# Dense products beside the delta rule, issued in portions of four chunks of a tile in place of two

## What is computed

```python
CHUNK, A_HEADS, A_DK, A_DV = 64, 8, 128, 128

def _gated_deltanet(q, k, v, alpha, beta, a_log, dt_bias):
...
    kk = jnp.einsum("bhncd,bhnjd->bhncj", k, k)
    L = jnp.where(strict, beta[..., :, None] * kk * decay, 0.0)
    rhs = jnp.concatenate([beta[..., None] * v, (beta * jnp.exp(G))[..., None] * k], axis=-1)
    sol = lax.linalg.triangular_solve(jnp.eye(CHUNK, dtype=f32) + L, rhs, left_side=True,
                                      lower=True, unit_diagonal=True)
    u_t, w = sol[..., :A_DV], sol[..., A_DV:]
...
    def step(S, inp):
        ut, wt, pt, qt, kt, et = inp
        U = ut - jnp.einsum("bhck,bhkv->bhcv", wt, S)
        o = jnp.einsum("bhck,bhkv->bhcv", qt, S) + jnp.einsum("bhcj,bhjv->bhcv", pt, U)
        S = S * et[..., None, None] + jnp.einsum("bhck,bhcv->bhkv", kt, U)
        return S, o
```

## Time and profile before

| | before |
|---|---|
| median of three runs (lowest, highest) | 2479.69 us (2476.96, 2483.39) |
| profiled execution, its own time | 2473.95 us |
| its span | 2472.3 us |
| busy: PE, PEld, DVE, ACT, POOL | 2425.7, 2004.9, 1007.0, 935.4, 1182.7 us |
| dense matmuls L1886, largest group (HH, WH) | 1992, 795.0 us |
| mean granted clock of TensorE | 0.993 of full |

### The profile page before, as it was taken

One profiled execution on the slowest core, in us unless ns is written; L12 is line 12 of the kernel. 1 busy time (PEld: TensorE's weight loads), 2 busy tenths in 40 slices (PEclk: granted clock), 3 DMA queues, 4 the chain that ended last, 5 costly groups with the idle time before them and its releaser, 6 DMA issues.

```text
span 2472.3 us, 35533 instructions
## 1 busy us (share of the span) xinstructions
PE 2425.7 (98%) x14295; PEld 2004.9 (81%) x14295; DVE 1007.0 (41%) x2261; ACT 935.4 (38%) x1435; POOL 1182.7 (48%) x1566
## 2 busy tenths in 40 slices
PE   8999999999999999999999999999999999999998
PEld 6888888888788888888888888877868887888887
DVE  7974211124874211123867774224345333211113
ACT  5553222224563322224544453235553344322221
POOL 5125655654115565655533233443326645655563
PEclk9999999999999999999999999999999999999999
DMA  5532223224632223224211111232213322223222
GB/s 177 139 103 86 102 88 109 99 77 130 164 103 86 103 81 115 85 85 141 94 58 53 53 52 53 81 133 86 69 58 128 116 96 79 96 86 110 103 80 83
DMA packets 42403, 237.17 MB, mean 96 GB/s; under 512 B 4736, under 2 KB 7936, under 8 KB 19712
## 3 DMA queue, kind: packets, MB, share of 16 engines
q1 hardware_dynamic: 39936, 218.13, 25.0%
q0 software_dynamic: 2304, 16.78, 3.3%
HBM read 213.92 MB, written 4.19 MB: 88 GB/s over the span
## 4 chain that ended last, share of the span: by engine, by line
PE 91%; DVE 4%; POOL 2%; issue 1%; ACT 1%; DMA 1%; SPq 0%; DVEq 0%; POOLq 0%; ACTq 0%
PE PB L1886 75%; PE PB L1888 4%; POOL WL L3028 1%; PE PB L1898 1%; PE PB L1923 1%; PE PB L2136 1%; PE PB L2117 1%; DVE cc L2614 1%; PE PB L1970 1%; PE PB L1987 1%; PE PB L2124 1%; DMA WR<-in_w_in 1%; PE PB L2148 1%; PE PB L2164 1%; PE PB L2087 0%
## 5 line engine op out<-in xcount | busy, mean ns | idle before, releaser
L3028 POOL TENSOR_TENSOR WL<-WR,WH 128x256 fp32r<-128x256 f32 (+1 forms) x1444 | 1055.0, 767 | 753.6 <-ACT WH L2183 753.6
L1886 PE MATMUL PB<-HH,WH 128*128 128x512 f32 x1992 | 795.0, 399 | 11.0 <-ACT HH L2198 10.5
L1886 PE MATMUL PB<-HL,WH 128*128 128x512 f32 x1992 | 779.4, 391 | 0.9 <-DVE HL L2506 0.9
L1886 PE MATMUL PB<-HH,WL 128*128 128x512 f32 x1992 | 516.5, 396 | 0.8 <-DMA WL<-WR 0.8
L2183 ACT ACTIVATE WH<-WR 128x2048 fp32r<-128x2048 f32 (+1 forms) x209 | 371.9, 1779 | 245.9 <-PE PB L1886 238.2
L1886 PEld LDWEIGHTS PB<-HH,WH 128*128 128x128 f32 x1992 | 375.8, 189 | 101.2 <-issue 13.7
L1886 PEld LDWEIGHTS PB<-HL,WH 128*128 128x128 f32 x1992 | 375.8, 189 | 76.9 <-issue 1.7
L1886 PEld LDWEIGHTS PB<-HH,WL 128*128 128x128 f32 x1992 | 366.4, 188 | 75.3 <-issue 2.0
L1886 PE MATMUL PB<-BL,WH 128*128 128x512 f32 (+1 forms) x859 | 331.6, 387 | 0.6 <-DVE BL L2515 0.6
L1886 PE MATMUL PB<-BH,WH 128*128 128x512 f32 (+1 forms) x795 | 307.9, 388 | 1.3 <-ACT BH L2218 1.3
L1886 PE MATMUL PB<-BH,WL 128*128 128x512 f32 (+1 forms) x795 | 195.0, 389 | 1.5 <-POOL WL L3028 1.5
(11 more groups left out here) (363 smaller groups left out, 2678.4 us busy)
## 6 DMA issues: line engine op xcount, KB each, us to landing
WR<-in_w_gu SPq DMA_DIRECT2D x66, 1024.0 KB, 4.7
WR<-in_w_dn SPq DMA_DIRECT2D x48, 704.0 KB, 4.0
WR<-in_w_in SPq DMA_DIRECT2D x22, 1024.0 KB, 4.8
WL<-WR POOLq DMA_DIRECT2D x16, 1024.0 KB, 6.9
WR<-in_qkv SPq DMA_DIRECT2D x12, 1024.0 KB, 4.7
WR<-in_w_out SPq DMA_DIRECT2D x8, 1024.0 KB, 4.7
WR<-in_qk SPq DMA_DIRECT2D x8, 1024.0 KB, 4.8
WR<-in_gb SPq DMA_DIRECT2D x4, 1024.0 KB, 4.7
```

Source lines behind the costliest of these rows:

```text
L1886: ins = pe.matmul(out[:, 0:n], wt[:, k * cols + j * P:k * cols + (j + 1) * P], x[:, k, t0:t0 + n], start=first, stop=last)
L3028: g.tensor_tensor(m.WL[u % 2][:, part], m.WR[u % 2][:, part], f32(m.WH[u % 2][:, part]), ALU.subtract).then_inc(sems["wlo"], 1)
```

## The change

The step of the yields becomes a variable. It is four chunks while the lanes of the delta rule are woven, and two everywhere else. Eight matmuls now lie between two yields of part 0, four in part 1. The instructions of the program are the same; their order on the engines changes, since `weave` comes to the lanes less often. Lines behind L552 carry a number higher by one, behind L1497 by three.

```diff
@@ -549,6 +549,7 @@
     o.units = units()
     pos = {"load": 0, "split": 0, "use": 0}
     hfree = [[]]
+    portion = [2]
@@ -585,7 +586,7 @@
         for i in range(a, b):
-            if fine and (i > a and (i - a) % 2 == 0 or part == 1 and i == a):
+            if fine and (i > a and (i - a) % portion[0] == 0 or part == 1 and i == a):
@@ -1494,8 +1495,10 @@
+        portion[0] = 4
         weave(clock, products(), 0.0, lane(gates(), preparations()), inversions(), scans(), gatings(), last_gating(), operands(),
               convolutions(), curves_b(), curves_a())
+        portion[0] = 2
```

## The result

| | before | changed |
|---|---|---|
| median (lowest, highest), 13 runs each | 2478.55 us (2474.19, 2483.39) | 2490.19 us (2482.05, 2492.54) |
| profiled execution, its own time | 2473.95 us | 2482.30 us |
| its span | 2472.3 us | 2481.0 us |
| mean granted clock of TensorE | 0.993 | 0.994 |

The change makes the kernel slower: ratio to before 1.0047, 95% interval 1.0037 to 1.0057; 11.6 us by the medians. Eleven of the thirteen runs of the changed kernel took 2487 us or more. The profiled one is one of the two quick ones, so its numbers show the places, and its total is short of the median.

What follows compares the result with a forecast made beforehand. PE carries 91% of the chain, losing time only in waits or at the low clock. Terms 6.7 + 0.85 + 2.6 + 1.2 - 0.1 - 0.65 = +10.6 us on the median 2479.69 gave 2490 us, range 2477 to 2498.

Steps and rivals of the forecast that it cites:

- Part 1: Delta rule stage: 27 fewer stretches of dense matmuls between small products gain 0 us (bounds -2.4 and 0).
- Part 2: Beside head 6's preparation: PE stalls in two pieces about the spread, uncovered and behind DVE's queue, +6.7 us.
- Part 3: Clock falls after thin PE work: 1.7 us for the stall, less 0.85 for the old fall, net +0.85 us.
- rival C: The clock costs more: a fall lying wholly on work costs 3.5 us instead of 1.7, total 2494; chance 0.15.
- Part 4: Second inversion: its first two products stand side by side, so PE waits for DVE before the second, +2.6 us.
- Part 5: Smaller waits: first inversion +1.2 us, third net -0.1, fourth inversion's 0.64 us wait goes.
- A: Waits only change places because DVE may run ahead of PE: 2483 to 2485 us; chance 0.33.
- B: Faster: double cover takes waits away, 10 us gain, 2470 us, if the head 6 wait is under some 2; chance 0.05.
- D: The change does nothing to the kernel's time; chance under 0.01.

Runs made afterwards that it cites:

- e8: The changed kernel with portions of eight chunks instead of four: 2532.04 us, ratio 1.0231 to the kernel before.
- e1: The changed kernel, with the first gate tile's 24 matmuls no longer held back until head 6 is prepared, only its result: 2487.67 us, ratio 1.0042.
- e5: e1 with the second gate condition (filters of head 7 done) also moved behind its tile's matmuls: 2480.76 us, ratio 1.0018.
- e2: The changed kernel with PT, QD, EL and head 6's root moved behind UU and SS on DVE: 2491.82 us, ratio 1.0055.
- e3: The changed kernel with 20 dense matmuls one place earlier at the start of the second inversion: 2489.53 us, ratio 1.0048.
- e9: e3 with three filter taps and one copy of head 4 moved behind SS on DVE: 2485.89 us, ratio 1.0041.
- e12: The kernel before with twelve dense matmuls one place earlier at the end of the third inversion: 2474.17 us, ratio 0.9985.
- e11: The changed kernel with portions of four until head 7's projections and of two from there on: 2493.82 us, ratio 1.0064.
- e6: The kernel before (portions of two) with both gate conditions moved behind their matmuls: 2477.83 us, ratio 1.0016.

## Why the prediction held, step by step

The forecast of 2490.0 us, 10.3 above the median it had, met 2490.19, 11.6 above the median of thirteen. The terms are compared on the two profiled executions, whose own times differ by 8.4 us:

- **Part 1 (0).** Not measured alone. The account of the stage leaves nothing for it: 10.3 us of idle time, and half of the 6.6 us by which PE is busier under the low clock (15.49 us in its three falls, 8.93 in the two of before), an estimate of 3.3, make up the 13.5. e8 made far fewer changes and gained nothing.
- **Part 2 (+6.7).** 6.24 us, in the two pieces and with the releasers named. The missing 20 matmuls of cover were the right cause, as e1 and e5 show. Incomplete was the path: only DVE's queue was followed, and e2 found the PSUM banks behind it.
- **Part 3 (+0.85 net, 1.7 for the stall).** The term that was mis-sized: in the whole stage work at the low clock cost 3.2 us more than before. The clock was at half for 13.6 us. From the L2090 at 1463.95 to the next at 1474.05 lie 10.1 us. The same work at full clock takes 5.4 by the timeline of before, from start to start: 0.44 and 0.39 for L2090 and L2099, 0.81 for the column sums, 0.35 and 0.31 for the first group of turns and the row spread, 0.81 for the second group of turns, 0.37 for L2081, 1.93 for eight dense matmuls. That is 4.7 us lost, more even than the 3.5 of rival C, whose mechanism was the true one: most of the fall lay on work. The Trainium skill, TensorE: Matmul & The Clock Gate, section "HAM oscillation", reckons half the throttled time; for 13.6 us that is 6.8, an estimate by the page's rule. Here 4.35 us of the fall (1459.6 to 1463.95) were wait, and half of the rest is 4.6, close to the measured 4.7. The rule fits what lies on work and not the whole fall.
- **Part 4 (+2.6).** 1.28 us before the second product, not 2.6, and below the 2 to 3 that were named as a sign of being right. The wait ahead of the first, which was said to stay at 1.53, grew to 2.92. Together +2.7: right by two errors that cancelled. TC was ready at 1317.04, yet PE started at 1317.99, when SS had ended: the product's PSUM bank was that of the L2090 which SS reads. The order of PE says so (s_scan_v is signalled by DVE's steps of the scan):

```
L2090 MATMUL PB3<-UU_107,KD0_116 128x128 [waits s_scan_v]
...
L2029 MATMUL PB3<-TC_126,UM_128 32x32 [waits s_invert_v,s_scan_v]
```

- **Part 5 (+0.45).** First inversion: 1.00 us for TC, 1.2 forecast. Third: 3.6 us of new waits forecast, 1.18 + 1.97 and two under 0.4 found; the largest was ACT's copy between the last two products, put at 0.7. The old loss there was put at 3.7 us, while its waits for DVE in the profile of before are only 0.52 + 1.10 + 0.60. Fourth: no wait for another engine, as said.

The waits of the stage came out at +10.3 us where the sum without the clock was 9.75. Part of that agreement is chance. The sum had no term for 0.9 us more at the stage's first wait (1.41 for a filter's input in place of 0.49) nor for 0.7 us at the end of the second inversion (ACT's copy), and the third inversion came out some 1.6 us above its forecast (new waits 3.7, old ones gone 2.2). Against these, the pauses of PE with no releaser, which the sum left as they were, are 1.4 us in the changed kernel where before has 3.0.

That the totals agree within 0.2 us is luck. The stage took 13.5 us more, not 10.6, and most of the difference is the clock term. This did not show in the total, since the clock behind the stage differs by several us between executions, and the median of three that the forecast started from was itself 1.1 us high. Eleven of the thirteen runs of the changed kernel had a mean clock of 0.988 to 0.992, against 0.994 in the profiled one; where they lost it, no profile shows. The rivals: A (the waits only change places) is refuted by the stall, though it describes e1, e3 and e9 well; B asked for a stall under 2 us and was off; D is out.

## To carry to other kernels

Work that covers the waits of other chains is a stock: a planner that hands it out in larger portions, or an edit that moves it forward, leaves a hole where the stream next stands before a condition, so look for that place first. In the three places tried, cover helped where the engine that releases the wait had idle time of its own over the stretch (DVE busy 5.4 of 9 us in e12, 16.3 of 22 in e1) and not where it was busy throughout (16.1 of 17 in e3). And when a wait is traced to one engine's queue, look also at who frees the bank that the waiting group writes (e2), and at what the engine itself waits for ahead of the step in question (e11).

## What the runs showed of the hardware

- A stall of 6 us among small products went with 13.6 us at 1.2 of 2.4 GHz, 0.69 over the 22 us about it. With dense matmuls in the stall and the same small products behind it (e1, e5) the clock over the same 22 us was 0.92. Most of the low clock thus came with the stall, not with the small products behind it.
- The same order does not get the same clock. e3 and the changed kernel have the same order from 1340 to 1455, and in 1400 to 1450 the clock was 0.90 in e3 and 0.97 in the changed kernel. The first product of the third inversion starts at 1397.6 and 1397.9, that of head 6's preparation at 1443.4 and 1439.2: e3 lost 4.5 us more on the way, 1.2 of them in a longer wait in front of the spread (1.45 against 0.27). The changed kernel's thirteen runs go from 2482.1 us (clock 0.995) to 2492.5 us (0.988). One profile of this kernel is no measure of a change of 10 us in the total, nor of the clock that a place gets in other executions.
- Groups of 64 32x32 products sometimes pause in their middle with nothing to wait for that the profile shows: 1.85 us behind the sixtieth in the kernel before at 1252.57, at the start of a fall of the clock, 1.60 us in e6, and 0.66 us in e12 at 1417.23 at full clock. The cause stays open.
